# Expert weights in 1,024-column blocks for pairs of rounds, and expert outputs put back in short format, in a two-block transformer kernel

## The reference, cut to what matters

```python
def moe_swiglu(xn, router, w_gu, w_down):
    logits = (xn @ router).astype(jnp.float32)
    top_v, top_i = lax.top_k(logits, TOP_K)            # 2 of 8 experts
    w = jax.nn.softmax(top_v, axis=-1)
    comb = jnp.sum(jax.nn.one_hot(top_i, N_EXPERTS, dtype=jnp.float32) * w[..., None], axis=-2)
    out = jnp.zeros_like(xn)
    for e in range(N_EXPERTS):
        out = out + comb[..., e:e + 1] * swiglu(xn, w_gu[e], w_down[e])
    return out
def swiglu(xn, w_gu, w_down):
    g, u = jnp.split(xn @ w_gu, 2, axis=-1)            # w_gu: 1024 x 7168, w_down: 3584 x 1024
    return (jax.nn.silu(g) * u) @ w_down
```

## Time and profile before

| what | value |
|---|---|
| median of 3 runs | 2374.26 us (2366.45 to 2377.89) |
| the profiled execution, its own time | 2368.06 us |
| its span, first to last instruction | 2366.2 us |
| mean granted TensorE clock, of full speed | 0.995 |
| TensorE busy | 2336.2 us (99%) |
| TensorE weight loads busy | 2087.8 us (88%) |
| VectorE busy | 1795.2 us (76%) |
| ScalarE busy | 1371.1 us (58%) |
| bytes moved | 566.89 MB, mean 240 GB/s |

### The profile page before, as it was taken

How to read it: one execution, slowest core, us unless ns; L and a number is a source line. 1 busy time by engine, 2 the same in 40 slices (tenths; PEclk the granted TensorE clock), 3 DMA queues, 4 the chain that set the end, 5 groups by cost and what they waited for, 6 DMA issues and landing times.

```text
span 2366.2 us, 33661 instructions
## 1 busy us (share of the span) xinstructions
PE 2336.2 (99%) x14460; PEld 2087.8 (88%) x14460; DVE 1795.2 (76%) x1833; ACT 1371.1 (58%) x1354; POOL 119.2 (5%) x94
## 2 busy tenths in 40 slices
PE   9999999999999999999999999999999999999999
PEld 8989999788878888888888888888889999889999
DVE  6856656766788888888888888887777676767766
ACT  5445445364567777777677767776555444645342
POOL 2001000001100000000000000000310001301000
PEclk9999999999999999999999999999999999999999
DMA  8645465463599999999999999998334555433553
GB/s 272 198 139 176 146 222 170 150 198 107 169 357 340 350 354 350 350 356 344 355 351 346 370 333 367 344 350 278 116 107 140 195 189 170 125 118 114 180 177 108
DMA packets 309786, 566.89 MB, mean 240 GB/s; under 512 B 12482, under 2 KB 137697, under 8 KB 309504
## 3 DMA queue, kind: packets, MB, share of 16 engines
q1 hardware_dynamic: 304848, 559.34, 67.9%
q10 hardware_dynamic: 4784, 5.35, 0.7%
HBM read 563.60 MB, written 1.05 MB: 239 GB/s over the span
## 4 chain that ended last, share of the span: by engine, by line
PE 86%; DVE 6%; DMA 4%; ACT 3%; issue 0%; POOL 0%; ACTq 0%; SPq 0%; DVEq 0%; POOLq 0%
PE bank L1041 21%; PE bank L823 15%; PE bank L1059 11%; PE bank L665 9%; PE bank L807 7%; PE bank L653 6%; PE bank L253 6%; DVE wL L205 3%; DMA raw<-in_od_moe_gu 3%; PE bank L675 3%; ACT wH L234 2%; PE bank L1392 2%; PE bank L639 2%; PE bank L1340 2%; DMA raw<-in_od_moe_down 1%; DVE arena L205 1%
## 5 line engine op out<-in xcount | busy, mean ns | idle before, releaser
L205 DVE TENSOR_TENSOR wL<-raw,wH 128x2048 fp32r<-128x2048 f32 (+4 forms) x550 | 1214.2, 2217 | 341.8 <-ACT wH L234 339.4
L234 ACT ACTIVATE wH<-raw 128x2048 fp32r<-128x2048 f32 (+4 forms) x550 | 1015.4, 1849 | 490.7 <-PE bank L823 104.9
L1041 PE MATMUL bank<-wH,ra 128*128 128x512 f32 x1792 | 577.5, 393 | 4.4 <-DVE wL L205 4.1
L1041 PEld LDWEIGHTS bank<-wH,ra 128*128 128x128 f32 x1792 | 336.5, 188 | 76.4 <-issue 5.5
L823 PE MATMUL bank<-ra,wH 128*128 128x256 f32 x2112 | 382.4, 283 | 2.7 <-DVE arena L226 2.7
L1041 PE MATMUL bank<-wL,ra 128*128 128x512 f32 x896 | 348.7, 389 | 0.0
L823 PEld LDWEIGHTS bank<-ra,wH 128*128 128x128 f32 x2112 | 329.5, 192 | 4.5 <-DVE arena L226 3.5
L823 PE MATMUL bank<-ra,wL 128*128 128x256 f32 x1056 | 298.8, 283 | 0.0
L1059 PE MATMUL bank<-wH,ra 128*128 128x512 f32 x896 | 287.3, 392 | 0.2
L665 PE MATMUL bank<-wH,ra 128*128 128x512 f32 (+2 forms) x800 | 220.7, 358 | 0.5 <-DVE ra L208 0.5
L823 PEld LDWEIGHTS bank<-ra,wL 128*128 128x128 f32 x1056 | 202.7, 192 | 0.0
(11 more groups left out here) (214 smaller groups left out, 2589.2 us busy)
## 6 DMA issues: line engine op xcount, KB each, us to landing
raw<-in_od_moe_gu SPq DMA_DIRECT2D x224, 1024.0 KB, 6.5
raw<-in_od_moe_down SPq DMA_DIRECT2D x112, 1024.0 KB, 6.6
raw<-in_ev_ffn_gu SPq DMA_DIRECT2D x22, 1024.0 KB, 5.1
raw<-in_ffn_w_gate SPq DMA_DIRECT2D x22, 1024.0 KB, 5.4
raw<-in_ffn_w_up SPq DMA_DIRECT2D x22, 1024.0 KB, 5.4
raw<-in_ffn_w_down SPq DMA_DIRECT2D x22, 1024.0 KB, 4.9
raw<-in_xa_wkv SPq DMA_DIRECT2D x16, 1024.0 KB, 5.3
raw<-in_od_pw_w SPq DMA_DIRECT2D x12, 1024.0 KB, 5.0
```

The costliest lines, as they stand in the source:

```text
L205: self.op.tensor_tensor(out, a, b, op).then_inc(*self.sig.up(name))
L234: self.op.activation(out, a, ACT.Copy, **kw).then_inc(*self.sig.up(name))
L1041: m = p.op.matmul(out[:, :], a, b, start=half == 0 and c == 0 and i == 0, stop=half == 1 and c == 3 and i == 2)
```

## The change

The unit of work is no longer a round but a unit u of `UNITS`: rounds (0,1), (2,3), (4,5) and (6,) of each expert, three double units and a single one. Gate and up weights of a double unit come in blocks of 256 rows by 1,024 columns (rows of 4 KB instead of 2 KB), four for gate and four for up, each still one megabyte and 12 matmuls, and each feeds the banks of both rounds. The single unit keeps its blocks. TensorE runs gate(u), the turns of all rounds of u-1, up(u), down of all rounds of u-1. For experts 0 to 6 the outputs are scaled and split into a high half (ScalarE) and a low half (VectorE) in the place of the gathered tokens, and `pe_mix_in` makes two short-format matmuls for each of the eight F32 ones; expert 7 stays as it was. The calls on ScalarE and VectorE are rewritten by unit. Cut to what matters:

```diff
+UNITS = [(e, tuple(range(f, min(f + 2, NRD)))) for e in range(NE) for f in range(0, NRD, 2)]
...
-        def moe_gu(e, f, which):
-            col0 = (FE if which == "up" else 0) + f * 512
-            for half in range(2):
-                rect(("moe", e, f, which, half), gu_w[e][half * 512:(half + 1) * 512, col0:col0 + 512], 512, 4)
+        def moe_gu(u, which):
+            e, fs = UNITS[u]
+            col0, wd = (FE if which == "up" else 0) + fs[0] * 512, 512 * len(fs)
+            k = 1024 // (2 * len(fs))
+            for i, tag in enumerate(self.unit_tags(u, which)):
+                rect(tag, gu_w[e][i * k:(i + 1) * k, col0:col0 + wd], wd, k // 128)
...
+        for u, (e, fs) in enumerate(UNITS):
+            self.pe_project(p, u, "gate", self.act)
+            if u:
+                for h in self.unit_rounds(u - 1):
+                    self.pe_hidden_turn(p, h)
+            self.pe_project(p, u, "up", self.dve)
+            if e and fs[0] == 2:
+                self.pe_mix_in(p, e - 1)
+            if 0 < u < last:
+                for h in self.unit_rounds(u - 1):
+                    self.pe_moe_down(p, h)
...
             for c in range(k):
                 xh, xl = gx[0][:, k * j + c], gx[1][:, k * j + c]
                 end = j == len(tags) - 1 and c == k - 1
                 for n, (q, out) in enumerate(zip(rounds, outs)):
                     ns = slice(n * 512, (n + 1) * 512)
                     for i, (a, b) in enumerate(passes(xh, xl, wh[:, c, ns], wl[:, c, ns])):
                         m = p.op.matmul(out[:, :], a, b, start=j == 0 and c == 0 and i == 0, stop=end and i == 2)
...
+                    hi, lo = (v[:, n, :] for v in self.picked(e))
+                    p.sum(out, [(hi, to), (lo, to)]).then_inc(*self.pe.up(("mix_in", e, n)))
...
+            up = self.unit_tags(u, "up")
+            self.act_blocks(a, up[0])
+            for q in self.unit_rounds(u):
                 if q > 1:
                     a.wait_ge(*self.dve.of(("htm", q - 2)))
                 a.wait_ge(*self.pe.of(("gate", q)))
                 a.do(("gs", q), self.gs[:, q % 2, :], self.ps(("gate", q))[:, :], ACT.Silu)
+            self.act_blocks(a, up[1])
+            if u:
+                for h in self.unit_rounds(u - 1):
+                    self.act_hidden(a, h)
...
+        for i in range(2):
+            a.cp(("y", e, i), self.picked(e)[0][:, 4 * i:4 * i + 4, :], self.banks[i][:, :].rearrange("p (c n) -> p c n", c=4), scale=scale)
...
+            for tag in self.unit_tags(u, "gate"):
+                self.dve_blocks(v, tag)
+            up = self.unit_tags(u, "up")
+            self.dve_blocks(v, up[0])
+            self.dve_blocks(v, up[1])
+            if u:
+                for h in self.unit_rounds(u - 1):
+                    self.dve_hidden(v, h)
+            for tag in up[2:]:
+                self.dve_blocks(v, tag)
...
+    def dve_unit_down(self, v, u):
+        e, fs = UNITS[u]
+        for f in fs:
+            self.dve_blocks(v, ("moe", e, f, "down", 0))
+            if e == NE - 1 and f == NRD - 2:
+                self.dve_hidden(v, NE * NRD - 1)
+            self.dve_blocks(v, ("moe", e, f, "down", 1))
+            if e and f == 0:
                 for n in range(8):
+                    self.dve_moe_add(v, e - 1, n)
...
+        for i in range(2):
+            hi, lo = (x[:, 4 * i:4 * i + 4, :] for x in self.picked(e))
+            v.wait_ge(*self.act.of(("y", e, i)))
+            v.stt(("y", e, i), lo, self.banks[i][:, :].rearrange("p (c n) -> p c n", c=4), scale, hi.bitcast(F32), ALU.mult, ALU.subtract)
```

More of the change, by code:

```diff
@@ L467, in moe_down @@
                 rect(("moe", e, f, "down", half), dn_w[e][at:at + 256, :], 1024, 2)
[L469 to L474, removed]
+        for u in range(len(UNITS) + 1):
+            if u < len(UNITS):
+                moe_gu(u, "gate")
+                moe_gu(u, "up")
+            if u:
+                for f in UNITS[u - 1][1]:
+                    moe_down(UNITS[u - 1][0], f)
         for l in range(2):
@@ L1000, in pe_moe @@
         self.pe_gather(p, 0)
[L1001 to L1012, removed]
+        last = len(UNITS) - 1
+        for u, (e, fs) in enumerate(UNITS):
[9 more added lines that the diff above has]
+                    self.pe_moe_down(p, h)
+            if e + 1 < NE and NRD - 2 in fs:
                 self.pe_gather(p, e + 1)
-            if q == NRD:
+            if e == 1 and fs[0] == 0:
                 self.pe_flag(p)
[L1016 to L1019, removed]
+        one, two = self.unit_rounds(last - 1)
+        self.pe_moe_down(p, one)
+        self.pe_moe_down(p, two, (0,))
+        self.pe_hidden_turn(p, NE * NRD - 1)
+        self.pe_moe_down(p, two, (1,))
+        self.pe_moe_down(p, NE * NRD - 1)
         p.span = (4, 8)
@@ L1026, in pe_hidden_turn, with pe_project @@
                      [self.htm[:, h % 2, x * 128:(x + 1) * 128] for x in range(4)], 128, self.dve, ("hv_lo", h))
-    def pe_project(self, p, e, f, which, sig):
-        q = e * NRD + f
-        out = self.bank(p, (which, q), self.act if which == "gate" else self.dve, ("gs" if which == "gate" else "htm", q))
+    def pe_project(self, p, u, which, sig):
+        e, rounds = UNITS[u][0], self.unit_rounds(u)
+        outs = [self.bank(p, (which, q), sig, ("gs" if which == "gate" else "htm", q)) for q in rounds]
         gx = self.picked(e)
-        for half in range(2):
-            tag = ("moe", e, f, which, half)
-            wh, wl = self.pe_block(p, tag, 4)
+        tags, k = self.unit_tags(u, which), 4 // len(rounds)
+        for j, tag in enumerate(tags):
+            wh, wl = self.pe_block(p, tag, k)
             for g in range(2):
@@ L1037, in pe_project @@
                     p.wait_ge(*(self.act, self.dve)[g].of(("gather", e, g, c0)))
[L1038 to L1042, removed]
+            for c in range(k):
+                xh, xl = gx[0][:, k * j + c], gx[1][:, k * j + c]
+                end = j == len(tags) - 1 and c == k - 1
+                for n, (q, out) in enumerate(zip(rounds, outs)):
+                    ns = slice(n * 512, (n + 1) * 512)
+                    for i, (a, b) in enumerate(passes(xh, xl, wh[:, c, ns], wl[:, c, ns])):
+                        m = p.op.matmul(out[:, :], a, b, start=j == 0 and c == 0 and i == 0, stop=end and i == 2)
+                    if n < len(rounds) - 1 and end:
+                        m.then_inc(*self.pe.up((which, q)))
+            m.then_inc(*self.pe.up(("block", self.index[tag]), *([(which, rounds[-1])] if j == len(tags) - 1 else [])))
     def pe_moe_down(self, p, h, halves=(0, 1)):
@@ L1049, in pe_moe_down @@
             for i in range(2):
-                self.wait_bank(p, i, (self.act, self.dve)[i], ("y", e, i))
+                self.wait_bank(p, i, *((self.act, ("y", e, 0)) if i == 0 and e == NE - 1 else (self.dve, ("y", e, i))))
         very_last = h == NE * NRD - 1
@@ L1790, in act_moe @@
         self.act_gather(a, 0)
[L1791 to L1796, removed]
+        last = len(UNITS) - 1
+        for u, (e, fs) in enumerate(UNITS):
+            for tag in self.unit_tags(u, "gate"):
+                self.act_blocks(a, tag)
+            up = self.unit_tags(u, "up")
+            self.act_blocks(a, up[0])
+            for q in self.unit_rounds(u):
                 if q > 1:
@@ L1800, in act_moe @@
                 a.do(("gs", q), self.gs[:, q % 2, :], self.ps(("gate", q))[:, :], ACT.Silu)
[L1801 to L1815, removed]
-                    a.cp(("y", pe_, 0), self.yev[:, 0, :], self.banks[0][:, :], scale=self.weight[:, pe_ % 2:pe_ % 2 + 1])
```

104 lines of the change are left out of this document (62 added, 42 removed).

## The result

| what | before | changed |
|---|---|---|
| median of four runs | 2374.36 us | 2402.86 us (2398.57 to 2410.53) |
| ratio, 95% interval | | 1.0136 (1.0115 to 1.0158) |
| the profiled execution, its own time | 2368.06 us | 2404.42 us |
| mean granted TensorE clock, of full speed | 0.995 | 0.989 |

What follows compares the result with a forecast made beforehand. TensorE was taken to bound the kernel, with 0.95 us of slack per block. Terms -10.7 - 0.7 + 18.9 + 8.3 + 1.6 + 1 = +18.4 us on the median 2374.26 gave 2392.7 us, range 2376 to 2406.

Steps and rivals of the forecast that it cites:

- The put-back: Putting back an expert's output on TensorE: 1.92 us instead of 3.45, seven times, -10.7 us.
- The two stops: TensorE waits 2.36 us before down in eight single units and 1.18 us behind the additions seven times.
- The additions: Eight additions on VectorE before the next gate block's low half stop TensorE 1.18 us, seven times, +8.3 us.
- the hidden halves: In single units VectorE makes hv_lo behind the second down block's low half; TensorE stands 2.36 us, eight times, +18.9 us.
- The same matmuls otherwise: Blocks, matmuls and columns keep their number; matmul spacing on TensorE stays 0.227 us.
- Scaling of both banks: ScalarE scales two banks before the next high half instead of one: 0.23 us, seven times, +1.6 us.
- The restart: First product group behind a turn takes 0.03 us longer; 24 fewer such restarts, -0.7 us.
- Wide rows: 4 KB rows for gate and up blocks instead of 2 KB: counted at nothing.
- A: Transfers fall behind, each late landing in double units is paid: +31.4 us, 2405.7; chance 0.10.
- B: Only the hidden halves stop TensorE, the additions do not: +10.1 us, 2384.4; chance 0.12.
- C: Transfers were the pace all along, so TensorE's stops are partly repaid: +11.9 us, 2386.2; chance 0.08.
- D: Matmuls of double units come closer together, 0.216 us apart: total -6.9 us, 2367.4; chance 0.08.

Runs made afterwards that it cites:

- e1: The changed kernel with both hidden halves of a single unit made before the low half of its last up block: 2370.60 us, ratio 0.9998.
- e2: The changed kernel with the eight additions one low half sooner on VectorE, between the third and fourth down block: 2395.61 us, ratio 1.0095.
- e4: The changed kernel with four unused F32 products of zeros on TensorE between up and down of each single unit: 2389.58 us, ratio 1.0079.
- e7: As e3, but gate and up blocks of double units cut as before, 512 by 512 with 2 KB rows: 2368.14 us, ratio 0.9990.
- e3: The changed kernel with the edits of e1 and e2 together: 2365.31 us, ratio 0.9975.
- e8: As e3, with the second bank scaled and split one block later, behind the next unit's first gate block: 2364.84 us, ratio 0.9953.
- e9: The kernel of e3 run again, beside e8 on the same chip: 2363.15 us, ratio 0.9949.
- e5: The kernel before with only the short-format put-back of experts 0 to 6, rounds and blocks as before: 2366.59 us, ratio 0.9986.

## Why the prediction was right or wrong

The forecast was 2392.7 us, the measured median is 2402.86: slower, as forecast, inside the range (2376 to 2406), and 10 us above the forecast. If the ratio is laid on the forecast's base it is 14 us above (1.0136 x 2374.3 = 2406.6), just beyond the upper end. A loss of 18.4 us was forecast, one of 32 measured.

**Right, with their sizes.** The put-back: 1.92 us forecast, 1.91 measured. The two stops, counted link by link from the way of a block: 2.36 forecast, 2.43 measured; 1.18 forecast, 1.25 measured. The additions and the hidden halves are the two places, and e1 and e2 took each away alone, e2 but for 0.3 us a time that moved into down. The same matmuls otherwise: a gate of a double unit takes 10.88 us for 48, 0.227 each. Scaling of both banks came to 0.33 instead of 0.23.

**The step that failed** is the term "the hidden halves in the single unit", 8 x 2.36 = +18.9. Its size is 31.0 us by the ledger, of which the stop is 20.6, and 33 by e1. It was priced as the time in which TensorE stands, and the text said "Behind TensorE's stop nothing else is late". Late was TensorE itself: 1.4 to 1.6 us of half clock behind six of eight stops, 9.4 us in all, and 0.13 us of restart behind each. The other 1.7 us are the stop's own length, most of it the longer stop of the eighth unit. e4 shows the clock's part by itself, where the stop stayed and the lower clock did not.

The restart was in reach, and a reading of the chain hid it. The prediction took it as 0.03 us, from 5.47 against 5.44; by starts the same products take 5.55, so 0.11, much the same as behind a wait.

For the clock, a granted clock of 1.00 in every stretch read the earlier trace rows was a statement about an engine that never stood, and it should have been named as something that the stops could end. The trace of the kernel before has such a place 12 us behind the expert stage, where TensorE did not even stand but made 32 products of two columns:

```profile
1644.57 3.63 PE L1280 MATMUL bank<-small,arena 128*128 128x2 f32 x32
1648.06 0.72 PE L665 MATMUL bank<-wH,ra 128*128 128x512 f32 x1
...
1649.00 1.06 PE L665 MATMUL bank<-wH,ra 128*128 128x512 f32 x2
```

Behind them products of 512 columns stand 0.43 us apart, and the granted clock from 1648.2 to 1650.2 is 0.50. In the term of the additions the same restart is missing, 1.0 us.

**Wide rows counted at nothing** was wrong too for the landing, in the other direction. The argument was that the blocks of down with their 4 KB rows land no faster than the rest. But down and gate/up blocks are issued at different places and stand in different company. The comparison that decides is the same megabyte of gate and up at two widths: 6.5 us in e7, 6.0 in e3. What time this gives is not shown: among the stops of the changed kernel it cannot be told apart, and e7 against e3, e8 and e9 points to a few microseconds only.

**The rivals.** A, transfers fall behind, came nearest in number (2405.7), by a mechanism that did not take place: ScalarE's waits for gate and up blocks fell from 83.2 to 45.2 us. B, only the hidden halves bite, falls by the seven stops of 1.25 us and by e2. C, transfers were the pace, is not borne out: all of TensorE's waits for blocks were 9.4 us before and are 10.9 besides the stops now, so the stops were not repaid, and e1 and e2 gave back all that the ledger has for them. D, matmuls closer together, falls by the spacing of 0.227. With both stops gone the remaining terms of the sum, -10.7 - 0.7 + 1.6 + 1 = -8.8 us or a ratio of 0.996, lie between the two comparisons of e3 (0.9975 and 0.9949).

## What to carry to other kernels

Price a stop of TensorE by three numbers: the time it stands, the restart behind it, and the products that may follow at half clock. Here they were 2.4, 0.1 and 1.6 us, the last behind six of eight, and eight stops cost 31 to 33 us instead of 19. Read restarts between the starts of matmuls, since a chain of waits begins its rows at modelled ends. When the order of a software pipeline is rewritten in larger units, count for each consumer how many low halves stand ahead of what it needs in the smallest unit, since the same code gives a double unit slack and a single unit none. Read a saving from the stage that it is in: e5's stage was 8.8 us shorter in its trace while its ratio shows 3, and the part that nobody changed varies by 8 us from one execution to the next.

## What the runs showed that I had not expected

- The clock fell to half behind stops of 2.43 us, five times of seven, and not behind those of 1.25 us. Two equal stops (before 1001.79 and 1520.56 us) went without it, and in e2 three of seven did; what sets them apart stays open.
- Four products of zeros, which compute nothing, made the kernel some 13 us faster, by keeping TensorE at work for most of a stop of unchanged length; 9.4 us of it is the lower clock by the ledger.
- Blocks of one megabyte landed 0.5 to 0.6 us sooner with 4 KB rows than with 2 KB rows, while those of down, whose rows did not change, landed later (6.6 before, 6.8 to 7.0 in most kernels).
